# A diffusion trunk step on one core: tokens in grid-column order before the first projection, norms in two token halves, windowed neighbourhood attention

## The reference, cut to what matters

```python
for l in range(2):
    x += 0.5 * gate0 * swiglu(modulate(rms_norm(x)))        # FFN, 2816 wide
    x += gate1 * mixer_l(modulate(rms_norm(x)))
    x += 0.5 * gate2 * swiglu(modulate(rms_norm(x)))        # FFN
y = rms_norm(x)
# mixer 0: 8 heads of neighbourhood attention + 8 heads of latent (MLA) attention
# mixer 1: retention, 4 heads, forward and backward
# neighbourhood attention of a latent token at (row, column c): all 8 rows, the 16 columns
#   from clip(c - 8, 0, 48), a bias per offset, plus 128 cached keys; other columns get -inf
```

## Time and profile before

| | |
|---|---|
| median of 3 runs | 3238.27 us (3233.11 to 3241.33) |
| the profiled execution's own time | 3244.05 us |
| its span, first to last instruction | 3242.2 us |
| PE busy, instructions | 3171.7 us (98%), 19680 |
| PEld busy | 2917.7 us (90%) |
| DVE / ACT / POOL busy | 1477.7 (46%) / 905.4 (28%) / 287.6 us (9%) |
| mean granted TensorE clock | 0.989 |
| share of the chain that ended last: PE / DVE / ACT / DMA | 90% / 3% / 2% / 2% |

### The profile page before, as it was taken

One profiled execution on the slowest core, in us unless ns is written; L12 is line 12 of the kernel. 1 busy time (PEld: TensorE's weight loads), 2 busy tenths in 40 slices (PEclk: granted clock), 3 DMA queues, 4 the chain that ended last, 5 costly groups with the idle time before them and its releaser, 6 DMA issues.

```text
span 3242.2 us, 48789 instructions
## 1 busy us (share of the span) xinstructions
PE 3171.7 (98%) x19680; PEld 2917.7 (90%) x19680; DVE 1477.7 (46%) x2313; ACT 905.4 (28%) x1279; POOL 287.6 (9%) x366
## 2 busy tenths in 40 slices
PE   8899999999999999999999999999999999999999
PEld 4899999976979999999999999868697876999999
DVE  3565634247654665624652525253443524422323
ACT  4122214234454312224212124222212222421222
POOL 1000001012001000001000001030301104000001
PEclk9999999989999999999999999999999999999999
DMA  8443422221101444422442222212121211122222
GB/s 210 151 170 132 156 78 65 86 70 25 61 1 53 149 163 136 162 82 75 160 152 75 102 69 84 84 59 72 65 72 65 79 68 36 65 78 78 72 72 72
DMA packets 84911, 300.25 MB, mean 93 GB/s; under 512 B 10399, under 2 KB 12735, under 8 KB 84000
## 3 DMA queue, kind: packets, MB, share of 16 engines
q1 hardware_dynamic: 57888, 206.77, 18.5%
q0 software_dynamic: 20704, 74.89, 8.1%
q10 hardware_dynamic: 6176, 16.54, 1.4%
HBM read 290.67 MB, written 8.44 MB: 92 GB/s over the span
## 4 chain that ended last, share of the span: by engine, by line
PE 90%; DVE 3%; ACT 2%; DMA 2%; issue 2%; POOL 1%; SPq 0%; ACTq 0%; DVEq 0%; POOLq 0%
PE ps L1227 36%; PE ps L1212 30%; PE ps L1366 11%; PE ps L1422 2%; PE ps L1588 2%; PE ps L1397 2%; PE ps L1597 2%; ACT tmp_g L507 1%; DMA ada<-in_ada 1%; PE ps L1410 1%; PE ps L1576 1%; DMA x<-in_xT 1%; PE ps L1243 1%; PE ps L1248 1%; DVE negmax L991 0%
## 5 line engine op out<-in xcount | busy, mean ns | idle before, releaser
L1227 PE MATMUL ps<-h,w 128*128 128x320 f32 x8640 | 1278.7, 310 | 19.1 <-DVE w L799 18.7
L1227 PEld LDWEIGHTS ps<-h,w 128*128 128x128 f32 x8640 | 1271.1, 188 | 25.1 <-DVE w L799 20.0
L1212 PE MATMUL ps<-g,w 128*128 128x320 f32 x5376 | 793.1, 309 | 1.5 <-DVE g L1173 1.5
L1212 PEld LDWEIGHTS ps<-g,w 128*128 128x128 f32 x5376 | 790.5, 188 | 2.2 <-issue 2.2
L799 DVE TENSOR_TENSOR w<-raw,w 128x1024 fp32r<-128x1024 f32 x383 | 460.8, 1224 | 288.6 <-ACT w L482 282.8
L482 ACT ACTIVATE w<-raw 128x1024 fp32r<-128x1024 f32 x207 | 216.3, 1060 | 562.6 <-PE ps L1212 457.9
L1366 PE MATMUL ps<-w,h 128*128 128x512 f32 x1596 | 368.5, 391 | 3.1 <-ACT rv L741 3.1
L1366 PEld LDWEIGHTS ps<-w,h 128*128 128x128 f32 x1596 | 298.0, 188 | 67.0 <-issue 4.7
L898 DVE TENSOR_TENSOR tmp_g<-tmp_s,ps 128x640 f32<-128x640 f32 x88 | 72.3, 821 | 598.3 <-ACT tmp_s L523 598.3
L819 DVE CUSTOM_DVE_ANT_0 prod<-ada,crow 128x1024 f32<-128x1024 f32 x256 | 298.5, 1219 | 17.5 <-DMA ada<-in_ada 17.4
L523 ACT ACTIVATE tmp_s<-ps 128x640 f32<-128x640 f32 x88 | 62.0, 705 | 846.2 <-PE ps L1227 846.2
(11 more groups left out here) (161 smaller groups left out, 1854.2 us busy)
## 6 DMA issues: line engine op xcount, KB each, us to landing
raw<-in_ws SPq DMA_DIRECT2D x383, 512.0 KB, 3.6
ada<-in_ada POOLq DMA_DIRECT2D x132, 512.0 KB, 3.9
ada<-in_ada ACTq DMA_DIRECT2D x6, 1024.0 KB, 16.9
rst<-in_state ACTq DMA_DIRECT2D x4, 1024.0 KB, 4.7
out_new_state<-rsx ACTq DMA_DIRECT2D x8, 512.0 KB, 2.7
bias<-rp_rep POOLq DMA_DIRECT2D x16, 224.0 KB, 4.3
x<-in_xT SPq DMA_DIRECT2D x1, 2560.0 KB, 25.6
crow<-in_crow POOLq DMA_DIRECT2D x1, 1024.0 KB, 6.0
```

The costliest lines, as they stand in the source:

```text
L1212: mm = pe.matmul(pair_half(pr, half, width), w2[:, slot, wi, at:at + cols], rhs(k, ri)[:, half * width:(half + 1) * width], start=(k == 0 ...
L1227: mm = pe.matmul(pair_half(pr, half), w2[:, n % RING, wi, k * P:(k + 1) * P], h2[:, k, ri, half * HT:(half + 1) * HT], start=(k == 0 and w ...
```

## The change

- The latent tokens are stored column by column of the grid (8 rows of a column together) from the input to the output projection of neighbourhood attention. The window of a block of 128 queries (16 columns) is then a contiguous run of 192 or 256 keys instead of 512 (`NA_WINDOW`), so a unit has 320 or 384 keys with the cached ones, three transposes and three value products (`NA_CHUNKS`). Values need 6 token tiles instead of 5 (`V_AT`). Going back to row order is done by strided access in `add_by_rows`, in the latents' high and low parts and in the rotary products.
- The bias comes from the host spread out as 8 x 128 x 256 values; `rp_rep` and its transfer are gone; POOL adds the mask in three pieces a head.
- Every attention unit of the first kind has two extra ("filler") matmuls of 512 columns on PE (`dense`), and four stand ahead of the first. The first unit's scores are issued between the blocks of the value projection.
- Norms run in two halves of 320 tokens. The last chunks of x before a norm (those from `MH[nn]`, 4 or 5, to 7) are projected half by half, first all first halves, then the second ones; statistics of half 0 are taken while PE is still at second halves; the next layer's first two tiles run by halves (`halves`). Statistics use 4 tiles of 80 tokens. ACT's scale-and-shift and high part become one instruction, DVE's two become scalar_tensor_tensor. All `keep_warm` but one (17 at the start) are gone. The next weight splits are moved into the norm (`early`, `between`).
- `crow` is loaded and passed through SiLU a second time after MLA attention, since its place is reused. The output leaves in 8 transfers, by halves.

```diff
-V_BANK = [2, 3, 4, 5, 0]
+V_BANK = [2, 3, 4, 5, 6, 7]
...
+V_AT = [0, NCTX, NCTX + 64, NCTX + 192, NCTX + 320, NCTX + 384]
+V_OF = [None, 0, 1, 2, 3, 5]
+NA_WINDOW = {1: (0, 192), 2: (64, 256), 3: (192, 256), 4: (320, 192)}
+NA_CHUNKS = {1: [(0, 0, 0, P), (64, 1, 64, P), (192, 4, 0, P)],
+             2: [(0, 1, 0, P), (128, 2, 0, P), (256, 4, 0, P)],
+             3: [(0, 2, 0, P), (128, 3, 0, P), (256, 4, 0, P)],
+             4: [(0, 3, 0, 64), (64, 5, 0, P), (192, 4, 0, P)]}
...
+MH = [5, 5, 4, 5, 5, 4, 5]
...
+        xs = place("x", (KD + 1) * T).rearrange("p (k t) -> p k t", k=KD + 1)
+        x_cols, x = xs[:, 1:KD + 1, :], xs[:, 0:KD, :]
...
+            def add_square(nn, k, h):
+                pool.wait_ge(sq_done, squared(nn, k, h or 0))
+                if summed(nn, k, h or 0) > 1:
+                    pool.wait_ge(sq_add, summed(nn, k, h or 0) - 1)
+                acc_sq, new_sq = ((tmp_q[:, i, :] if h is None else half_of(tmp_q[:, i, :], h)) for i in range(2))
+                pool.tensor_tensor(acc_sq, acc_sq, new_sq, ALU.add).then_inc(sq_add, 1)
...
                 if nn:
...
+                    for k in range(1, MH[nn]):
+                        add_square(nn, k, None)
+                    for k in range(MH[nn], KD):
+                        add_square(nn, k, 0)
+                else:
+                    pool.wait_ge(const_ld, 144)
+                half_pow(nn, 0)
+                if nn:
+                    pool.wait_ge(n_diag, 2 * nn + 1)
+                    for k in range(MH[nn], KD):
+                        add_square(nn, k, 1)
+                half_pow(nn, 1)
...
-            pool.dma_start(a["rp_rep"].rearrange("r (e w) -> r e w", w=RPW),
-                           a["rpb"].rearrange("r (o w) -> r o w", o=1).to_broadcast([NAH * RPR, RP_REP, RPW])
-                           ).then_inc(rp_rep, 16)
+            row_load()
...
+                pool.wait_ge(rows_ld[h % 2], 16 * (h // 2 + 1))
...
+                for b, n0, n1, m0 in ((1, 8, 32, 0), (2, 0, 32, 24), (4, 0, 24, 56)):
...
+                    ins = pool.tensor_tensor(dst, r3[:, n0:n1, :],
+                                             colmask[:, m0:m0 + n].rearrange("p (n o) -> p n o", o=1)
+                                             .to_broadcast([P, n, ROWS]), ALU.add)
+                ins.then_inc(bias_rdy, 1)
             pool.wait_ge(s_mm, 2 * NU)
+            row_load()
+            pool.wait_ge(pv_mm, 2 * NU)
             ada_until(8 * 8, 8 * 8 + ADA_RING)
...
+                if nn:
+                    for k in range(MH[nn], KD - 1):
+                        norm_sq(k, nn, ready, 1)
+                        if k == MH[nn]:
+                            between()
+                for h in range(2):
+                    for k in range(KD if l is not None else 0):
+                        act.wait_ge(n_u, chunk(nn, h, k))
+                        for c0, c1, st in half_parts(h):
+                            ins = act.activation(h2[:, k, 0, c0:c1], tmp_u[:, k % 4, c0:c1], ACT.Identity,
+                                                 bias=mod[:, NMOD * l + 3 * s, k, st:st + 1])
+                        ins.then_inc(h_hi, 1)
+                        if nn and h == 0 and k == 2:
+                            norm_sq(KD - 1, nn, ready, 1)
+                    if nn and l is None and h == 0:
+                        norm_sq(KD - 1, nn, ready, 1)
+                    if nn and h == 0:
+                        early()
...
             n0 = EM_AT
...
                     if k < KD:
-                        if 8 * nn + k >= 2:
-                            dve.wait_ge(n_h, 8 * nn + k - 1)
-                        dve.tensor_tensor(tmp_s[:, k % 2, :], x[:, k, :], pair(2), ALU.mult).then_inc(n_u, 1)
-                    if k >= 1:
-                        dve.wait_ge(h_hi, 8 * nn + k)
-                        dve.tensor_tensor(h2[:, k - 1, 1, :], tmp_g[:, (k - 1) % 2, :],
-                                          h2[:, k - 1, 0, :].bitcast(fp32), ALU.subtract).then_inc(h_lo, 1)
+                        if k >= 4:
+                            dve.wait_ge(h_lo, chunk(nn, h, k - 4))
+                        for c0, c1, st in half_parts(h):
+                            ins = dve.scalar_tensor_tensor(tmp_u[:, k % 4, c0:c1], xn[:, k, c0:c1], amul[:, k, st:st + 1],
+                                                           pair(2)[:, c0:c1], ALU.mult, ALU.mult)
+                        ins.then_inc(n_u, 1)
+                    if k >= 2:
+                        dve.wait_ge(h_hi, chunk(nn, h, k - 2))
+                        for c0, c1, st in half_parts(h):
+                            ins = dve.scalar_tensor_tensor(h2[:, k - 2, 1, c0:c1], tmp_u[:, (k - 2) % 4, c0:c1],
+                                                           mod[:, NMOD * l + 3 * s, k - 2, st:st + 1],
+                                                           h2[:, k - 2, 0, c0:c1].bitcast(fp32), ALU.add, ALU.subtract)
+                        ins.then_inc(h_lo, 1)
+                    if k in after:
+                        after[k]()
...
+            def norm_tail(nn, add1, between, lines, early):
+                add1(MH[nn])
+                half_var(nn, 0)
+                between()
+                if MH[nn] == 4:
+                    add1(5)
+                half_diag(nn, 0)
+                add1(6)
+                lines(0, {2: lambda: add1(KD - 1), 5: lambda: half_var(nn, 1), 7: lambda: half_diag(nn, 1)})
+                lines(1, {3: early})
...
+            def add_by_rows(m, pr, g, count):
+                dve.wait_ge(x_upd, count - 1)
+                dve.scalar_tensor_tensor(ctx_of(x[:, m, :]), ctx_of(pair(pr)), g[:, m, 0:1], ctx_of(x_cols[:, m, :]),
+                                         ALU.mult, ALU.add)
+                dve.scalar_tensor_tensor(by_rows(lat_of(x[:, m, :])), by_columns(lat_of(pair(pr))), g[:, m, 1:2],
+                                         by_columns(lat_of(x_cols[:, m, :])), ALU.mult, ALU.add).then_inc(x_upd, 1)
...
+                    dve.tensor_tensor(by_rows(rope_tmp[64:96]), by_rows(lat_of(pq[96:128])),
+                                      by_columns(rope_mla[96:128]), ALU.mult)
+                    link(dve.tensor_tensor(by_rows(lat_of(qb[64:96, h, :])), by_rows(lat_of(pq[64:96])),
+                                           by_columns(rope_mla[64:96]), ALU.mult))
...
+                for i in range(NS):
+                    at = h * HT + i * ST
+                    mm = pe.matmul(ps[0:ST, 6 + h, i:i + 1], tmp_q[:, 0, at:at + ST], ones[:, 0:1],
+                                   start=True, stop=True, skip_group_check=True)
+                mm.then_inc(st_mm, 1)
...
+            def half_rb(nn, h):
+                pe.wait_ge(n_diag, 2 * nn + h + 1)
+                pe.matmul(pair_half(2, h), ones[0:ST, :], hdiag[0:ST].rearrange("p t c -> p (t c)"),
+                          start=True, stop=True).then_inc(n_rb, 1)
+            def halves(ns, prs, nn):
+                for h in range(2):
+                    for k in range(KD):
+                        if nn and h == 0 and k == 3:
+                            half_sum(nn, 1)
+                        if nn and h == 0 and k == KD - 1:
+                            half_rb(nn, 1)
+                        pe.wait_ge(h_lo, chunk(nn, h, k))
+                        for n, pr in zip(ns, prs):
+                            for wi, ri in ((0, 0), (0, 1), (1, 0)):
+                                mm = pe.matmul(pair_half(pr, h), w2[:, n % RING, wi, k * P:(k + 1) * P],
+                                               half_of(h2[:, k, ri, :], h), start=(k == 0 and wi == 0 and ri == 0),
+                                               stop=(k == KD - 1 and wi == 1))
+                            if h and k == KD - 1:
+                                mm.then_inc(wt_free, 1)
...
+                                pe.wait_ge(x_upd, xb + 8 * r + m - 2)
+                                have(n)
+                            half_tile(n % RING, m % 3, of_g, h, nf).then_inc(wt_free if h else dn_half, 1)
+                            if h and m == mh:
+                                half_sum(NORM_AFTER[q], 0)
+                            elif h and m == KD - 2:
+                                half_rb(NORM_AFTER[q], 0)
+                    if q == 3:
+                        half_sum(6, 1)
+                        half_rb(6, 1)
...
+                    w0, nw = NA_WINDOW[b] if na else (0, NLAT)
+                    sc_out = bank2(g % 2)
+                    pe.matmul(sc_out[:, 0:nw], lhs, lat_of(k[:, PAST:])[:, w0:w0 + nw], start=True, stop=True)
+                    mm = pe.matmul(sc_out[:, nw:nw + PAST], lhs, k[:, 0:PAST], start=True, stop=True)
                 mm.then_inc(s_mm, 1)
...
-                for kt in range(1 if b == 0 else 5):
-                    mm = pe.transpose(bank2(2)[:, kt * P:(kt + 1) * P], src[:, kt * P:(kt + 1) * P], ident)
```

(39 more changed lines are left out.)

586 lines of the change are left out of this document (371 added, 215 removed).

## The result

The changed kernel takes 3194.56 us (median of 4 runs, 3193.57 to 3197.34), the kernel before 3235.69 in runs beside it (4 runs, 3232.69 to 3241.33): ratio 0.9872, 95% interval 0.9855 to 0.9889. That is 41 us faster, where 84 were forecast, and 4.6 us above the top of the range. By the two profiled executions the span falls by 50.3 us, from 3242.2 to 3191.9. The 9 us between these two figures lie in the two executions that were profiled: that of before took 8 us more than the median of its runs (5.8 more than the median that the prediction knew), that of the changed kernel 1 us less.

A forecast was written before the change was run, and what follows sets the result against it. TensorE's chain was taken as the bound, its FFN pieces unchanged, gains lying between them. Start -11, norms -43, attention with values -30 sum to -84: 3244.05 to 3160, 5.8 less against the median: 3154 us; range 3128 to 3190.

The forecast's parts named there:

- Norms 2 and 5: Half-norms after the output projections: losses of 27.3 and 22.8 us fall to 14.6 and 11.9, gains of 12.7 and 10.9.
- the new wait for POOL: In norms 2 and 5, squares of half 0 finish 3 us after PE asks for their statistics.
- Attention: First attention, units with fewer keys: 91 us against 128.9, -38; net with the values -30.
- Rival 1: Attention stays bound by its chain (score, DVE, ACT, DVE, PE), half-norms gain three quarters: 3178 us; chance 0.18.
- Strides: Strided operands, as in mixer 0's rotary products on DVE, taken as free: no cost in the sum.
- rival 3: Strided operands at half rate: 16 rotary products cost 0.53 us more each, about 4 us, 3158; chance 0.11.
- The rule of the Trainium skill: Rotary products: fp32 steps beyond 4 elements cost, here the step is 8; sum some 4 us worse, -80.
- the wait at the start: Before 106.22, PE's 13.6 us wait goes with the `rp_rep` transfer; net -11 after 2.5 us of costs.
- norms 1, 3 and last: Half-norms: norms 1 and 3 together -10 us, the last norm -2.
- the values: Mixer 0's value projection: 24 more matmuls cost 5.5 us, and banks the latents' norm still reads cost 2.
- Norm 4: Half-norm before retention: loss falls from 17.0 to 9.6 us, -7.5.
- rival 4: Clock slower than before, at 0.50 in the new attention and the norms' halves: 3294 us; chance 0.05.

The follow-up runs named there:

- run 5: The changed kernel with PE also signalling the first tile of each pair of whole tiles in the output projections before norms 2 and 5: 3188.8 us, 0.9849.
- run 6: The kernel of run 5 plus matmuls whose result nobody reads (8 and 5) in PE's waits of norms 2 and 5: 3185.1 us, 0.9837.
- run 7: The kernel of run 5 with the second SiLU of the condition rows moved behind the first up tile's SiLU of FFN 1: 3182.0 us, 0.9830.
- run 1: The kernel before the change, with only the rp_rep transfer issued behind the adaLN rows of FFN 0: 3224.9 us, 0.9971.
- run 4: The changed kernel with every value product of the first attention over 128 rows of keys, none cut to 64: 3191.9 us, 0.9852.
- run 8: The changed kernel with the rotary table of mixer 0's queries copied once into row order, so rotary products have no strided operand: 3188.8 us, 0.9850.
- run 2: The changed kernel with only the attention unit's fillers changed: none 3227.2 us, both ahead of the transposes 3194.5 us, one 3186.5 us.

## Why the prediction fell short

- **Norms 2 and 5** are the step that failed. First, their old losses of 27.3 and 22.8 us were wrong. I took the end of the chain's piece (994.53+21.34 = 1015.87) for the end of the output projection. The chain leaves PE there, for POOL's sums of squares; PE itself had two of its eight tiles still to do. The timeline of PE in the kernel before says so, for norm 2 and for norm 5:

```profile
1013.78 9.11 PE L1212 MATMUL ps<-g,w 128*128 128x320 f32 x61
1022.73 3.29 PE L1243 MATMUL ps<-ident 128*128 128x128 f32 x28
...
2715.51 29.80 PE L1212 MATMUL ps<-g,w 128*128 128x320 f32 x192 [1.46 <-DVE g L1173]
2745.15 3.29 PE L1243 MATMUL ps<-ident 128*128 128x128 f32 x28
```

From 1022.7 on, 1057.29-1022.7-14.1 = 20.5 us were lost, and by the same reading some 7 less than I wrote in norm 5 too: 14 us of the forecast gain never existed. Counting matmuls would have shown it: 8 tiles of 24 are 192, and the piece has 144. Second, the new wait for POOL was forecast at 3 us and is 4.6, since I let the whole tiles' squares run at their own pace and did not see that tiles are released two by two (run 5). Third, I counted nothing for the clock behind that wait, though I had named a slow clock in the waits in the bounds; the 24 matmuls alone lose 1.7 us in norm 2 and 2.3 in norm 5 (run 6), and the 12 behind them 1.2 more in norm 5. Fourth, the second SiLU, forecast at 3.5 us, is worth 4.6 with the clock (run 7). The small rest is argued and not tested: DVE's first low part, forecast for the moment that PE can use it, is 1.5 and 1.0 us later, and the output projection ahead of norm 5 runs its first matmuls slowly. The sum for norm 5 also has 11.9 us where its terms give 11.1.
- **Attention**: the mechanism was right, PE packed and the clock at 1.00, though the gain of 29.2 us is against one trace of before (run 1's would give 26). The mis-sized term is a head's own work: I had 4x1.93+0.70 = 8.4 us, the trace of a head has 9.8, of which the value products are most: 4.0 for 3.2, about half of it through the changes between 64 and 128 rows (0.4 us a head in run 4), the rest not parted further; the transposes take 0.48 a unit for 0.41. Ten fillers are 2.6 us, near the 2.3 forecast. 1.7 us a head are 14 us; start-up and stalls, set at 5.4, were 0.5 (99.7 less 8x12.4). Rival 1 is out: with two fillers DVE's chain is hidden; it begins to show with one.
- **Strides**: taken as free, at 0.53 us a product and 4 us in rival 3; measured 0.46 to 0.50 and 4.8 (run 8), the whole of what was lost in that stretch; the strided adds to x took 1.23 us instead of 0.74 but cost the kernel nothing. The rule of the Trainium skill that I set against the change (SBUF — State Buffer, Door 1: The DMA port swizzle) was right here: the 8-element step costs, and the trace agrees with it in sign. The page gives no price. That the row of before had no strided operand was no reason to take zero.
- **Right**: the wait at the start and its cause (run 1), norms 1, 3 and last within 2.4 us, the values. The start gave 4.9 us more, since the matmuls behind the old wait had lost 2.3 us to the clock and the edits charged at 2.5 cost next to nothing. Norm 4 gave 3.8 us more: the 96 matmuls behind its old wait took 17.02 us and take 14.08 now. So the missed price of the clock behind a wait worked both ways, and part of what the norms lost came back here by luck. The clock (rival 4) did not fall in the attention; run 2 shows that this hangs on the fillers.

## What to carry to other kernels

Where a piece of the chain ends is where the chain leaves an engine, not where the engine ends: count its instructions before a loss is reckoned from it. An overlap is worth what its first wait leaves: look at how often the producer signals, and at the clock behind each wait, in the old kernel as in the new one. Where the clock comes and goes, look for an effect in every trace that has the place, not in one pair. A filler should be tried at half its number and half its length, since what it holds (here the clock, 31 us) may be had for less (here for 8 us less).

## What the runs showed of the hardware

- In the attention without fillers the granted clock went from 1.00 to 0.50 (2.4 to 1.2 GHz) after PE had stood 0.3 to 0.8 us in most of the units since 684, never longer, and PE's unbroken work from 700 to 800 did not raise it again. The same units with one filler each, and waits of 0.3 to 0.6 us, stayed at 1.00.
- After a wait of PE of 1.9 to 4.6 us in norms 2 and 5, 24 matmuls of 320 columns took 5.2 to 6.3 us in 18 cases of 18; with eight matmuls in the wait 3.77 in 6 of 6. Behind the waits of about 1 us that follow, 12 matmuls took 2.3 us in half of the 18 and 3.2 to 3.6 in the others, behind much the same waits; what decides it is not shown.
- A DVE product of 512 columns whose table steps 8 elements takes 1.18 us, 0.70 without the step. A plain DVE copy of 512 columns with the same step took 0.68 (run 8).
- Of three value products, one on 64 rows between two on 128 costs 0.28 us more than three on 128.
